# Query and key rows of the sparse attention stored without their norm, and multiplied by it when they are read back

## What is computed

```
def rms_norm(x, g):
    x32 = x.astype(jnp.float32)
    y = x32 * lax.rsqrt(jnp.mean(x32 * x32, axis=-1, keepdims=True) + NORM_EPS)
    return y.astype(x.dtype) * g
...
def sparse_attention_branch(qc, kc, vc, zc, iq, ik, iw, q_norm, k_norm, cos_a, sin_a, cos_i, sin_i):
    b, t, _ = qc.shape
    q = apply_rope(rms_norm(qc.reshape(b, t, SA_HEADS, SA_HEAD_DIM), q_norm), cos_a, sin_a)
    k = apply_rope(rms_norm(kc.reshape(b, t, SA_HEADS, SA_HEAD_DIM), k_norm), cos_a, sin_a)
...
    logits = jnp.einsum('bqhd,bqkhd->bhqk', q_b.astype(jnp.float32), k_sel.astype(jnp.float32)) * (SA_HEAD_DIM ** -0.5)
```

## Time and profile before

| | us |
|---|---|
| median of 3 runs | 1934.23 (1933.93 to 1934.9) |
| profiled execution | 1935.43 |
| its span | 1933.6 |
| PE busy | 1915.2 |
| DVE, ACT, POOL busy | 1220.3, 935.6, 709.7 |

### The profile page before, as it was taken

One profiled execution on the slowest core, in us unless ns is written; L12 is line 12 of the kernel. 1 busy time (PEld: TensorE's weight loads), 2 busy tenths in 40 slices (PEclk: granted clock), 3 DMA queues, 4 the chain that ended last, 5 costly groups with the idle time before them and its releaser, 6 DMA issues.

```text
span 1933.6 us, 25166 instructions
## 1 busy us (share of the span) xinstructions
PE 1915.2 (99%) x9658; PEld 1549.1 (80%) x9658; DVE 1220.3 (63%) x2106; ACT 935.6 (48%) x1433; POOL 709.7 (37%) x534
## 2 busy tenths in 40 slices
PE   9999999999999999999999999999999999999999
PEld 6878878877788878787877787777766788989989
DVE  6767755555745668656464737665544447878787
ACT  6455553343345465544334345577555445444343
POOL 5545432433455454432434455546322354000000
PEclk9999999999999999999999999999999999999999
DMA  5434542423534235632423545422211333323231
GB/s 202 128 120 128 141 136 71 165 74 114 194 104 173 98 115 147 161 99 74 156 75 135 181 144 157 154 92 79 77 55 55 111 106 111 121 76 121 87 110 66
DMA packets 94791, 227.70 MB, mean 118 GB/s; under 512 B 29937, under 2 KB 34033, under 8 KB 93361
## 3 DMA queue, kind: packets, MB, share of 16 engines
q1 hardware_dynamic: 88752, 222.95, 35.0%
q10 hardware_dynamic: 5920, 3.15, 0.7%
HBM read 193.95 MB, written 24.64 MB: 113 GB/s over the span
## 4 chain that ended last, share of the span: by engine, by line
PE 80%; DVE 11%; ACT 3%; DMA 2%; issue 1%; POOL 1%; SPq 1%; ACTq 0%; DVEq 0%
PE bank L466 79%; DVE ER L400 1%; DVE kv L400 1%; PE bank L470 1%; SPq L395 1%; DVE tmp L400 1%; POOL wl L400 1%; DMA X<-inverses 1%; DMA gt<-gates 1%; DVE scs L425 1%; DMA kv<-blocks 1%; ACT wh L455 1%; DVE tmp L410 1%; DVE m8s L422 0%; ACT lt L452 0%
## 5 line engine op out<-in xcount | busy, mean ns | idle before, releaser
L400 POOL TENSOR_TENSOR wl<-st,wh 128x512 fp32r<-128x512 f32 x490 | 660.6, 1371 | 855.3 <-ACT wh L455 855.2
L466 PE MATMUL bank<-hh,wh 128*128 128x512 f32 x1616 | 651.1, 403 | 2.4 <-DVE hl L410 0.5
L466 PE MATMUL bank<-hh,wl 128*128 128x512 f32 x1616 | 629.2, 390 | 0.0
L466 PE MATMUL bank<-hl,wh 128*128 128x512 f32 x1616 | 628.9, 390 | 0.0
L455 ACT ACTIVATE wh<-st 128x1024 fp32r<-128x1024 f32 (+1 forms) x302 | 316.7, 1050 | 171.6 <-PE bank L466 129.3
L466 PEld LDWEIGHTS bank<-hh,wh 128*128 128x128 f32 x1616 | 303.3, 188 | 89.6 <-issue 24.3
L466 PEld LDWEIGHTS bank<-hl,wh 128*128 128x128 f32 x1616 | 303.7, 188 | 67.2 <-issue 6.9
L466 PEld LDWEIGHTS bank<-hh,wl 128*128 128x128 f32 x1616 | 303.3, 188 | 64.4
L400 DVE TENSOR_TENSOR xt<-xt,bank 128x512 f32<-128x512 f32 x80 | 54.9, 686 | 116.0 <-PE bank L466 116.0
L466 PE MATMUL bank<-fh,wh 128*128 128x256 f32 x448 | 126.9, 283 | 0.3 <-DVE xt L400 0.3
L466 PE MATMUL bank<-fl,wh 128*128 128x256 f32 x448 | 126.8, 283 | 0.0
(11 more groups left out here) (363 smaller groups left out, 3025.6 us busy)
## 6 DMA issues: line engine op xcount, KB each, us to landing
st<-units SPq DMA_DIRECT2D x300, 512.0 KB, 3.5
gates<-tmp SPq DMA_DIRECT2D x48, 256.0 KB, 2.8
gt<-gates SPq DMA_DIRECT2D x48, 256.0 KB, 3.6
pads<-tmp SPq DMA_DIRECT2D x32, 128.0 KB, 2.9
qk<-tmp SPq DMA_DIRECT2D x16, 256.0 KB, 4.3
x_scratch<-xt SPq DMA_DIRECT2D x2, 2048.0 KB, 9.0
xt<-x_scratch SPq DMA_DIRECT2D x2, 2048.0 KB, 8.7
ph<-phi SPq DMA_DIRECT2D x8, 512.0 KB, 4.6
```

Source lines behind the costliest of these rows:

```text
L400: return NOTHING if self.e is None else self.e.tensor_tensor(out, a, b, op)
L466: return NOTHING if self.e is None else self.e.matmul(out, lhsT, rhs, start=start, stop=stop, skip_group_check=share)
```

## The change

Rows are stored rotated but without their norm. Square of row c goes into one of four tiles, `L.sq` = `nacc`, `nr` and two new ones that lie where `L.mix` of the delta rule was. After row 3 and after row 7, PE does one `sums` into bank 3, ACT one root for four heads (with the scale 1/128) into `nacc` and its copy in `fp32r` into `L.rmix`, and DVE one `mixed`. `L.rmix[0]` is `gx` of the delta rule, `L.rmix[1]` is new. In `front3` PE does a `spread` behind the tiles zc 1 and zc 3, and DVE multiplies `qs` and then `ks` in place from banks 4 to 7. The waits that this needs are in the diff; the load of `qs` has a semaphore of its own now.

```
         L.gx = sb(f"gx{l}", [128, T], F32R, stack=dtmp)
+        L.rmix = [L.gx, sb(f"rmix{l}", [128, T], F32R, stack=dtmp)]
...
+        sb(f"dr_heads{l}", [128, 24 + 13 * 1024 + 8 + 640], stack=dr)
+        L.sq = [nacc, nr] + [sb(f"rsq{i}{l}", [128, T], stack=dr) for i in range(2)]
...
             def row(c):
                 yield
-                pe.wait_ge(*at("qk_sq", l, c))
-                pe.mm(bank(3, "qk_mean", l, c), mean, row_tiles(c)[2][:], True, True).then_inc(*sig("qk_mean", l, c))
+                if c % 4 == 3:
+                    pe.wait_ge(*at("qk_sq", l, c))
+                    sums(3, layer[l].sq, "qk", l, c // 4)
...
             for c in range(4):
                 yield from tile(("p", l, 4616 + 128 * c), c, ("zc", l, c), g)
+                if c % 2 == 1:
+                    spread(L.rmix[c // 2], "qk", l, c // 2)
                 yield
...
-                    pe.wait_ge(*at("p3_in", l, "ks"))
+                    pe.wait_ge(*at("free7", "qk_row", l, 1, 3))
                     pe.mm(o[:, 0:nk], L.qs[:, h, sq4(b)], L.ks[:, h, 0:nk], True, True).then_inc(*sig("sp_s", l, n))
...
                 ac.wait_ge(*at(f"free{b}", "qk", l, c))
-                ac.act(x2[:], x[:], ACT.Square).then_inc(*sig("qk_sq", l, c))
-                yield
-                ac.wait_ge(*at("qk_mean", l, c))
-                rnorm(x2[:], banks[3][:], 3, ("qk_mean", l, c), "qk_r", l, c)
+                if c == 2:
+                    ac.wait_ge(*at("dn_up", l, 1))
+                if c == 4:
+                    ac.wait_ge(*at("qk_mix", l, 0))
+                ac.act(L.sq[c % 4][:], x[:], ACT.Square).then_inc(*sig("qk_sq", l, c))
+                yield
+                if c % 4 == 3:
+                    ac.wait_ge(*at("qk_mm", l, f))
+                    rnorm(nacc[:], banks[3][:], 3, ("qk", l, f), "qk_r", l, f, scale=1.0 / 128.0)
+                    ac.wait_ge(*at("qk_r", l, f))
+                    if f == 0:
+                        ac.wait_ge(*at("h_g", l, 3))
+                    ac.cp(L.rmix[f][:], nacc[:]).then_inc(*sig("qk_hi", l, f))
                 yield
...
-                dv.tt(x[:], x[:], xs, ALU.add).then_inc(*sig("qk_n", l, c, 2))
-                dv.wait_ge(*at("qk_n", l, c, 2))
-                dv.wait_ge(*at("qk_r", l, c))
-                dv.tt(x[:], x[:], x2[:], ALU.mult).then_inc(*sig("qk_o", l, c))
+                dv.tt(x[:], x[:], xs, ALU.add).then_inc(*sig("qk_o", l, c))
+                if c % 4 == 3:
+                    yield
+                    mixed(layer[l].rmix[c // 4], nacc, "qk", l, c // 4)
...
                 twice_silu(L.zc[:, c, :], tmp[c], c, "zc", l, c)
+                if c >= 2:
+                    f = c - 2
+                    dv.wait_ge(*at("qk_up", l, f))
+                    dv.wait_ge(*(at("p3_in", l, "ks") if f else at("qs_in", l)))
+                    for h in range(4):
+                        x = (L.qs, L.ks)[f][:, h, :]
+                        dv.tt(x, x, banks[4 + h][:], ALU.mult).then_inc(*sig(f"free{4 + h}", "qk_row", l, f, h))
...
-            sp.dma(L.qs[:], qk_d[:, 0:4, :]).then_inc(*dma("p3_in", l, "qs"))
+            sp.dma(L.qs[:], qk_d[:, 0:4, :]).then_inc(*dma("qs_in", l))
```

More of the change, by code:

```diff
@@ L309 @@
 SHARED = {
-    "pe_heads": "dn_mm tp gl h_g h_kk dn_up on_up h_w h_kv h_r h_uw sc_w sc_s sc_o on_mm",
-    "pe_rows": "norm_mm qk_mean q2_mm k2_mm pl_mm lru_mm",
+    "pe_heads": "dn_mm tp gl h_g h_kk dn_up on_up qk_up h_w h_kv h_r h_uw sc_w sc_s sc_o on_mm",
+    "pe_rows": "norm_mm qk_mm q2_mm k2_mm pl_mm lru_mm",
     "pe_attend": "sel_mm sp_s sp_t sp_o ns_s ns_t ns_o cm_s cm_t",
@@ L316 @@
     "act_heads": "dn_hi on_hi dn_sq dn_r on_sq on_r egl gexp h_eg h_dt h_vb h_xt",
-    "act_rows": "pl_p qk_sq qk_r q2_sq q2_r k2_sq k2_r conv_0 conv2_0 conv_th zc_a pl_a ga_a gelu_a rec_a",
+    "act_rows": "pl_p qk_sq qk_r qk_hi q2_sq q2_r k2_sq k2_r conv_0 conv2_0 conv_th zc_a pl_a ga_a gelu_a rec_a",
     "act_attend": "sel_r sp_e ns_e cm_e gs_a",
@@ L322 @@
     "dve_heads": "dn_mix g_hi g_mix h_e h_n h_k vn0 sc_e inv",
-    "dve_rows": "qi ki qk_n qk_o q2_n q2r k2_n k2r rope conv_v conv2 gelu rec_v",
+    "dve_rows": "qi ki qk_n qk_o qk_mix q2_n q2r k2_n k2r rope conv_v conv2 gelu rec_v",
     "dve_attend": "top sel sp_r sp_n ns_r ns_n cm_v cm_n",
@@ L857, in row_tiles @@
     def row_tiles(c):
-        return tmp[c % 2], pad[c % 2][:, 16:16 + T], (nacc, nr)[c % 2]
+        return tmp[c % 2], pad[c % 2][:, 16:16 + T]
     def conv_tiles(c):
@@ L1640, in row @@
             def row(c):
-                b, (x, _, x2) = row_bank(c), row_tiles(c)
+                L, b, f, x = layer[l], row_bank(c), c // 4, row_tiles(c)[0]
                 ac.wait_ge(*done("p", l, 3080 + 128 * c))
@@ L2279, in index_q @@
             def index_q(c):
-                x, xs, _ = row_tiles(c)
+                x, xs = row_tiles(c)
                 yield
@@ L2285, in row @@
             def row(c):
-                x, xs, x2 = row_tiles(c)
+                x, xs = row_tiles(c)
                 w = "q" if c < 4 else "k"
```

## The result

| | us |
|---|---|
| after, median of 6 runs | 1949.46 (1947.08 to 1951.27) |
| before, median of 6 runs beside them | 1934.08 (1933.63 to 1935.62) |
| ratio after to before | 1.0076, 95% interval 1.0066 to 1.0086 |
| predicted | 1943.6, range 1937.2 to 1947.0 |

The change makes the kernel 15 us slower. The direction was as predicted, the size was not: 9.4 us were forecast, and the time lies above the range. The profiled execution took 1950.28 us, with a span of 1948.5; its granted clock is 0.994 in the mean where the kernel before has 1.0.

What follows compares the result with a forecast made beforehand. PE bounds the kernel, with DVE late ahead of the inverses' DMA. X0 shifts of 3.3 and 1.6, 0.5 behind them and 4.0 for the clock sum to +9.4 us on 1934.23: 1943.6 us, range 1937.2 to 1947.

Steps and rivals of the forecast that it cites:

- the added wait: Row 4's Square on ACT waits for DVE's query mix; PE stands still 7.3 us ahead of row 5's tile (T3).
- the shift at the X0 products: Products on the inverted blocks start later: +3.3 us in layer 0, +1.6 in layer 1, before 2.0 per layer for the clock.
- row 0's product: Mean product ahead of PE's wait for `kf`: removing it gains nothing, since the 1.21 us wait stays.
- copy of layer 0: Layer 1: everything 569.9 us later than in layer 0, but X0 products began 571.6 later before, hence +1.6 us.
- The bound: PE, busy 1915.2 of 1933.6 us; gains ahead of the X0 products count only if the inverses' DMA comes earlier.
- PE's own work: 14 of 16 removed mean products count, 12.2 us off; `sums` and `spread`s add 7.3: PE's work falls by 4.9 us.
- row 1's product: Its removal ahead of the DVE chain in the projections starts that chain 0.9 us earlier, at 179.7.
- The clock after the stop: Behind the stop ahead of row 5's tile, PE loses 2.0 us per layer at half rate, +4.0; ends 0 and 5.4 per layer.
- Behind the X0 products: Row 6's product and a bank wait go, row 7's becomes `sums`, two `spread`s come: +0.25 us per layer, +0.5 together.
- Rival 2: Longer stop, or late copies of XT ahead of the X0 products, 1 to 1.5 us more per layer: 1946; chance 0.12.
- Rival 3: The mix comes early enough that ACT doesn't stop ahead of row 5's tile: 1931.8, not slower; chance 0.09.
- Rival 4: Nothing waits anywhere and PE's own sum holds: -4.9 us, 1929.3; chance 0.04.

Runs made afterwards that it cites:

- rot: Changed kernel with key rows using the four square tiles one place further round, so ACT waits for the mix only before row 7's Square: 1941.78 us, ratio 1.0031.
- rot_short: `rot` with the last 7 of 31 inversion steps left out on DVE, so it computes another thing: 1931.47 us, ratio 0.9980 to the kernel before.
- top_rot_fill: `rot_fill` with the first top-k's rounds six steps later on DVE, three of six pairs behind the inversion: 1928.69 us, ratio 0.9969 to the kernel before.
- top_before: Kernel before with only the first top-k's rounds moved six steps later on DVE, three of six pairs behind the inversion: 1931.67 us, ratio 0.9988.
- fill: Changed kernel with one unread ones-product on row 0's square put back ahead of PE's wait for `kf` in each layer: 1946.97 us, ratio 1.0064.
- after_again: The changed kernel run once more, nothing altered, beside other runs on one chip: 1948.93 us, ratio 1.0069 to the kernel before.
- stop_filled: Changed kernel with unread 128x512 products, 26 in layer 0 and 36 in layer 1, filling PE's stop ahead of row 5's tile: 1943.76 us, ratio 1.0043.
- rot_fill: `rot` with one unread ones-product on row 0's square ahead of PE's wait for `kf` in each layer: 1938.90 us, ratio 1.0025 to the kernel before.
- rot_fill_later: `rot_fill` with the delta rule's heads, X0 products included, one side-stream step later on every engine: 1946.08 us, ratio 1.0053 to the kernel before.
- before_later: Kernel before with only the delta rule's heads one side-stream step later on every engine: 1941.42 us, ratio 1.0026.
- rot_best: `rot` with the queries' mix behind the inversion's end on DVE and small fillers in the waits for `kf` and at the X0 products: 1934.47 us, ratio 0.9997.
- code_shift: Changed kernel with 26 unread 16-column products in layer 0's stop ahead of row 5's tile, shifting PE's later code by 52 instructions: 1948.81 us, ratio 1.0064.

## Why the prediction was right or wrong

The mechanism held: the added wait on ACT stops PE ahead of T3, and the clock falls behind the stop. The step that failed is the size of the shift at the X0 products, 5.3 us in layer 0 and 3.6 in layer 1 with the clock, which measured 6.6 and 8.0 in the profiled execution. Two terms behind it were wrong: row 0's product was priced at nothing, and layer 1 was taken for a copy of layer 0.

- **The bound.** Right, and it decided most: gains ahead of the X0 products are lost unless the inversion on DVE ends earlier. `rot` shows it as a wait of 3.39 us, `rot_short` by its absence in layer 0, and `top_rot_fill` by a time 3 us under `top_before`.
- **PE's own work.** Predicted -4.9 us. That the busy sum of `rot` is 4.9 lower too is chance: it counts row 0's products as gone and holds two stretches at half the clock. At full clock and with something in row 0's place, `top_rot_fill` has 6.9 us less than `top_before`: 4.9, the 1.0 of the `ki,qi` products that the prediction has as a term of its own, 0.4 for the `sums`, each 1.08 us across (193.88 to 195.19 in `rot`, less 0.23) for 1.19, and 0.6 that I can't place. But the 0.9 us by which row 1's product was to bring the DVE chain forward failed: PE came earlier to `qf,kf` and waited 0.77 us for DVE's `lT`, in both layers. It was no gain for the same reason as row 0's.
- **Row 0's product.** "Hides in a wait that stays", priced at nothing. Here a step failed that I never took: I asked what the product cost, not what it did for the wait. It kept the idle time at 1.21 us; without it PE idled 2.08 us, and eight matmuls in layer 0 and seven in layer 1 ran at half the clock, some 1.5 us lost in each. In layer 0 1.2 of it reached DVE's chain: its first operation behind this wait came at 144.44 for 143.44 although PE had reached the wait for `kf` 0.3 us early. The other traces bear it out: counted from the layer's first `spread`, `qf,kf` starts at 27.8 us wherever the clock held behind a bare wait for `kf`, in the kernel before as in those with the strips, and at 29.0 to 29.1 in the eight places where it fell. `fill` was 1 to 2 us under the changed kernel by the ratios, within the noise.
- **The added wait.** Mechanism, queue and places right; the mix at 222.74 for 221.8, T3 at 227.78 for 226.8, PE idle for 6.6 us, for 7.3. The mis-sized term is the start of the chain: 181.35, not 179.7, for the two reasons above. From there to the mix DVE took 41.4 us, for 42.1, so POOL's stretching and the two multiplications gave back somewhat more than counted.
- **X0 products.** +6.6 us in layer 0 for 5.3 with the clock: 1.0 from the late T3, 0.3 from the clock. +8.0 in layer 1 for 3.6. That is the largest miss: T3 came 2.35 us later than layer 0's timing gives (1.3 of it the late blocks), 1.0 as in layer 0, and the clock cost 0.7 more than counted; 0.3 are left. Its size differs between executions: in the profiled one of `after_again`, 3.4 us shorter, the same shift was +6.6 in layer 0 and +3.9 in layer 1. I had taken layer 1 for a copy of layer 0 shifted in time; it is one in the program, but not in how DMAs and loads of code meet.
- **The clock after the stop.** Predicted 2.0 us per layer from the start of the kernel; 12 matmuls at the low rate made 2.3 (227.78 to 232.89, less 12 x 0.227 and 0.1), 14 made 2.7 in layer 1. `stop_filled` priced the two at 5.2 together. Hence the Trainium skill's sentence (TensorE: Matmul & The Clock Gate, section Why this matters for your kernels) that idle gaps between bursts bring the engine to half rate holds here. The page means longer gaps than 2.08 us, behind which the clock fell in 8 of 14 cases; here the measurement decides. The 18 stops of 1.21 us at the same place in nine kernels were never followed by it.
- **Behind the X0 products.** Predicted +0.25 per layer, measured +0.2 and 0.0. The `spread`s cost 1.3 us a layer as predicted (6.8 for 5.5 us of delay across them), nothing waits at `qs`, `ks` or the sparse products, the `ki,qi` product paid 0.92 and not 1.44, and 24 table loads are gone.
- **The rivals.** Rival 2's time (1946) came nearest. Of its two mechanisms, late copies of XT aren't in the trace, since the X0 products waited for nothing; the longer stop is there in layer 1, 8.93 us for 7.3. Rival 3 (ACT not stopped) was priced at 1931.8; as `rot` it made 1941.8 and with fillers 1934.5. It counted no low clock at all: the profiled run of `rot` has it in layer 1 behind `kf` and behind a stop of 1.82 us, that of `rot_fill` at the X0 products of both layers. Rival 4 (1929.3, PE's sum holds) has nearly the time of `top_rot_fill`, 1928.7, but by chance: 2.8 us of that gain are the order on DVE, and the strips gave 3.0, not 4.9.
- **The range** ended at 1947.0 since I took the clock's price as known and counted only one place for it. With a low clock possible behind each stop of some 2 us or more, of which there were four, the upper end should have been some 1950.

## What to carry to other kernels

Before a result that many instructions share is written to a tile that the next row needs, look which engine reads it last and how late that engine runs; here another order of the same four tiles, at no cost, took the stop away. A cheap instruction ahead of a wait may be what keeps PE's clock up: when it is taken out, price the wait as bare idle time, and fill it with work of full width: one full-precision product of 512 columns was enough at every wait for `kf` here. When an engine is made faster ahead of a join with a DMA, look in the queue of the engine that ends the other branch for work that nobody waits for yet (here three pairs of top-k rounds, 5.7 us): moving it was worth about as much as the strips.

## What the runs showed of the hardware

- The granted clock fell to 0.50 behind stops of PE of some 2 us, but not each time: the stop of 2.08 us was followed by five to eight matmuls at 0.43 us or by none, a stop of 3.4 us by none in `rot` and by slow X0 products in `rot_fill`; one of 1.82 us by seven in layer 1 of `rot`, while the earlier trace rows has one of 1.82 us with nothing behind it. Of the five of 1.92 us in `rot_fill_later` and `before_later`, three were followed by a stretch at the low clock. Times scatter with it: `rot` took 1937.3 us at a mean clock of 0.998, and 1939.6 to 1942.6 at 0.996. Behind the stops of 6.6 us and more it fell every time.
- 26 products of 64 columns back to back over 2.8 us didn't keep the clock in layer 1 of `rot_best`, though PE was never idle; in layer 0 it stayed full behind them. Products of 512 columns kept it in both layers of `stop_filled`. The 26 products of 16 columns in `code_shift` took 2.8 us too.
- A load of code (16 KB on q8) that began 1.2 to 2.4 us behind the issue of the blocks' transfer went with 0.9 to 1.4 us of delay, in eight kernels of eight. Adding 26 small products in another place moved the load away, and the delay with it.
